# HGRN: the differences of the cumulated log forgets of all eight levels are made by GpSimd in a program of its own

## What is computed

```python
G = jnp.cumsum(gc, axis=2)                       # cumulated log forgets
o_inter = einsum('bhtk,bhkv->bhtv', qc * exp(G), state)
diff = G[:, :, :, None, :] - G[:, :, None, :, :]
decay = exp(where(causal, diff, -inf))
scores = einsum('bhtk,bhsk,bhtsk->bhts', qc, kc, decay)
o_intra = einsum('bhts,bhsv->bhtv', scores, vc)
new_state = exp(G_last) * state + einsum('bhsk,bhsv->bhkv', kc * exp(G_last - G), vc)
```

## Time and profile before

| | before |
|---|---|
| median of three runs | 1599.02 us (1597.28 to 1599.33) |
| span of the profiled execution | 1598.3 us |
| PE busy | 1431.5 us, 90% |
| VectorE busy | 1088.6 us, 68% |
| ScalarE busy | 668.1 us, 42% |
| GpSimd busy | 177.5 us, 11% |
| mean granted clock of TensorE | 0.923 of 2.4 GHz |
| HGRN levels | 1281 to 1353 us of the span |

### The profile page before, as it was taken

The page is one execution under the profiler, slowest core; times in us unless marked ns, Lnnn a source line. Parts: engine busy times, 40 slices in busy tenths (PEclk is TensorE's granted clock), DMA queues, the critical chain, the costliest instruction groups (busy, mean ns, idle before and its releaser), DMA issues.

```text
span 1598.3 us, 19161 instructions
## 1 busy us (share of the span) xinstructions
PE 1431.5 (90%) x6855; PEld 1189.2 (74%) x6855; DVE 1088.6 (68%) x1058; ACT 668.1 (42%) x747; POOL 177.5 (11%) x271
## 2 busy tenths in 40 slices
PE   1876769999799999996899999999998798899998
PEld 1775557888678888774678888788888787778886
DVE  4678774777658886657467775678866698555554
ACT  0433224444254434544353444534446744344442
POOL 1101220111121110210011110211101000100000
PEclk9887778999889999995789999999999899889999
DMA  7741644999468994550168995689954433066671
GB/s 298 259 167 46 229 148 158 310 322 322 155 234 307 342 337 172 185 184 0 53 211 269 315 312 179 223 279 355 336 201 132 146 117 105 27 197 210 211 231 71
DMA packets 183523, 333.96 MB, mean 209 GB/s; under 512 B 8634, under 2 KB 122911, under 8 KB 182322
## 3 DMA queue, kind: packets, MB, share of 16 engines
q1 hardware_dynamic: 157040, 237.95, 44.4%
q0 software_dynamic: 26112, 95.07, 16.6%
q10 hardware_dynamic: 322, 0.27, 0.1%
HBM read 330.64 MB, written 2.62 MB: 209 GB/s over the span
## 4 chain that ended last, share of the span: by engine, by line
PE 73%; DVE 16%; ACT 4%; DMA 3%; issue 2%; POOL 1%; ACTq 0%; DVEq 0%; POOLq 0%
PE ps L1462 67%; DVE wlo L878 2%; DMA ada_raw<-in_w_ada 2%; PE ps L1580 2%; DVE ada_acc L1401 1%; POOL st L415 1%; DVE ada_acc L1027 1%; PE ps L1534 1%; ACT xn L562 1%; DVE xn L943 1%; PE ps L1515 1%; ACT xn L565 1%; DVE ada_acc L897 1%; PE ps L1665 1%; PE ps L1608 1%
## 5 line engine op out<-in xcount | busy, mean ns | idle before, releaser
L878 DVE TENSOR_TENSOR wlo<-raw,whi 128x2048 fp32r<-128x2048 f32 x215 | 490.2, 2285 | 166.0 <-ACT whi L525 166.0
L525 ACT ACTIVATE whi<-raw 128x2048 fp32r<-128x2048 f32 x215 | 409.7, 1909 | 264.1 <-PE ps L1462 241.7
L1462 PE MATMUL ps<-whi,hhi 128*128 128x512 f32 (+1 forms) x1208 | 486.5, 403 | 22.5 <-DVE wlo L878 7.9
L1462 PE MATMUL ps<-wlo,hhi 128*128 128x512 f32 (+1 forms) x1208 | 476.3, 394 | 0.0
L1462 PE MATMUL ps<-whi,hlo 128*128 128x512 f32 (+1 forms) x1208 | 476.2, 394 | 0.0
L1462 PEld LDWEIGHTS ps<-whi,hhi 128*128 128x128 f32 x1208 | 231.2, 191 | 76.5 <-issue 15.7
L1462 PEld LDWEIGHTS ps<-whi,hlo 128*128 128x128 f32 x1208 | 230.7, 191 | 49.3
L1462 PEld LDWEIGHTS ps<-wlo,hhi 128*128 128x128 f32 x1208 | 231.2, 191 | 47.4 <-issue 1.4
L897 DVE SCALAR_TENSOR_TENSOR ada_acc<-ada_raw,csil,ada_acc 128x1024 f32<-128x1024 f32 x120 | 150.4, 1278 | 12.7 <-DMA ada_raw<-in_w_ada 10.3
L1462 PE MATMUL ps<-whi,ahi 128*128 128x512 f32 x400 | 156.1, 390 | 0.0
L1462 PE MATMUL ps<-whi,alo 128*128 128x512 f32 x400 | 155.7, 389 | 0.0
(11 more groups left out here) (233 smaller groups left out, 1387.8 us busy)
## 6 DMA issues: line engine op xcount, KB each, us to landing
raw<-in_ffn_w_in SPq DMA_DIRECT2D x176, 512.0 KB
ada_raw<-in_ada_w POOLq DMA_DIRECT2D x96, 512.0 KB, 5.3
raw<-in_ffn_w_down SPq DMA_DIRECT2D x44, 1024.0 KB
big<-in_ada_w POOLq DMA_DIRECT2D x48, 512.0 KB, 6.7
ada_raw<-in_w_ada POOLq DMA_DIRECT2D x32, 512.0 KB, 4.6
raw<-in_hgrn_w_in SPq DMA_DIRECT2D x16, 1024.0 KB
raw<-in_attn_w_qkv SPq DMA_DIRECT2D x12, 1024.0 KB
raw<-in_w_gate SPq DMA_DIRECT2D x22, 512.0 KB
```

The costliest lines, as they stand in the source:

```text
L525: sc.activation(whi[:, slot, 0:n], raw[:, slot, 0:n], ACT.Copy).then_inc(w_hi, 1)
L878: ve.tensor_tensor(wlo[:, slot, 0:n], raw[:, slot, 0:n], whi[:, slot, 0:n].bitcast(F32), ALU.subtract)\
L1462: done = pe.matmul(dst, lhsT, rhs, start=first and n == 0, stop=final and n == 2, skip_group_check=True)
```

## The change

DVE's function `differences` and its calls are removed. GpSimd gets a function of the same name with the same subtractions, the same places, the same waits (`k_ready`, `lv_mm`) and the same signal (`lv_sub`); it makes all eight levels one after another, behind the set-up of the scan and ahead of the roots of the output norm. Where DVE linked the first two subtractions of level 8, GpSimd does so by a semaphore `lv_first`.

```diff
+            def differences(level):
+
+                E = decayed(level)
+                if level == 1:
+                    pool.wait_ge(k_ready, 2)
+                if level >= 3:
+                    pool.wait_ge(lv_mm, 2 * (level - 1))
+                if level <= len(LEVELS):
+                    n = LEVELS[level - 1]
+                    e, g = halves(E, level), halves(h_G, level)
+                    middle = g[:, :, 0, n - 1:n].to_broadcast((P, HEADS * TOK // (2 * n), n))
+                    done = pool.tensor_tensor(e[:, :, 0, :], middle, g[:, :, 0, :], ALU.subtract)
+                    if level > 1:
+                        done = pool.tensor_tensor(e[:, :, 1, :], g[:, :, 1, :], middle, ALU.subtract)
+                else:
+                    e, g = (a.rearrange("p h (c n) -> p h c n", n=CHUNK) for a in (E, h_G))
+                    total = [g[:, :, c, CHUNK - 1:CHUNK].to_broadcast((P, HEADS, CHUNK)) for c in range(3)]
+                    pool.tensor_tensor(e[:, :, 0, :], total[0], g[:, :, 0, :], ALU.subtract).then_inc(lv_first, 1)
+                    pool.wait_ge(lv_first, 1)
+                    pool.tensor_tensor(e[:, :, 0, :], e[:, :, 0, :], total[1], ALU.add)
+                    pool.tensor_tensor(e[:, :, 1, :], total[1], g[:, :, 1, :], ALU.subtract)
+                    done = pool.tensor_tensor(e[:, :, 3, :], g[:, :, 3, :], total[2], ALU.add)
+                done.then_inc(lv_sub, 1)
+
...
                     pool.memset(flat[:, 0:2 * TOK:CHUNK], 0.0).then_inc(scan_set, 1)
+                    for level in range(1, len(LEVELS) + 2):
+                        differences(level)
                     for t in range(NT):
                         reciprocal_root(sums_v, sums_before(6) + 1 + t, 120 + 8 * t, 8, P, EPS2)
...
                 forget(1)
-                differences(1)
                 lo(U + 9)
                 lo(U + 10)
                 for level in range(len(LEVELS) + 2):
                     if level:
                         decay(level)
                         take_scores(level - 1)
-                        if level <= len(LEVELS):
-                            differences(level + 1)
                     if level <= 7:
                         lo(U + 11 + level)
```

More of the change, by code:

```diff
@@ L271, in two_blocks @@
         q_copied, vg_out, lv_sub, lv_exp, lv_mul = sem("q_copied"), sem("vg_out"), sem("lv_sub"), sem("lv_exp"), sem("lv_mul")
-        lv_mm, lv_copy, g_silu = sem("lv_mm"), sem("lv_copy"), sem("g_silu")
+        lv_mm, lv_copy, g_silu, lv_first = sem("lv_mm"), sem("lv_copy"), sem("g_silu"), sem("lv_first")
         def linked(engine, own):
```

## The result

| kernel | median | runs from to | profiled span | granted clock |
|---|---|---|---|---|
| before (four runs) | 1598.77 us | 1597.28 to 1599.33 | 1598.3 us | 0.923 |
| changed (four runs) | 1608.88 us | 1608.62 to 1610.13 | 1607.0 us | 0.922 |

The changed kernel takes 1.0063 times as long, with a 95% interval of 1.0047 to 1.0079. That is 10.1 us more, beyond the 3.2 us that a measurement of this kernel can tell from no change: slower.

A forecast was written before the change was run, and what follows sets the result against it. PE and DVE were both taken as full in each 9.1 us level. Idle time 8.7 plus clock 4.05 less tail 1.3 gave +11.45 us on 1599.0, so 1610.5 us; forecast's own range 1605 to 1616, overall 1597.3 to 1618.

The forecast's parts named there:

- idle time at levels 2, 4 and 6: PE ahead of scores(2), (4), (6): waits twice the GpSimd price less 1.2, 2.9 us each, 8.7 in all.
- Two full engines: Levels 1 to 7: PE (9.13 us) and DVE (9.12) both full, so removing DVE work alone gains nothing there.
- Exclusive reading: GpSimd reads and DVE's two-SBUF-input instructions exclude each other; DVE waits for the whole GpSimd instruction, in order of asking.
- The price: One 128x1024 subtraction on GpSimd: 2.05 us taken, bounds 1.03 and 3.1 us.
- Who asks first: Level 2: GpSimd asks at 1288.4, DVE's multiplies at 1289.0, so GpSimd goes first; scores(2) at 1296.8 instead of 1293.89.
- the alternation: Levels 2, 4 and 6 each lose 2.9 us; at level 3 GpSimd's reads fall beside masked copies, without delay.
- The end: Level 8: without four half differences on DVE, level 7's masked copy starts at 1347.6 instead of 1348.97; gain 1.3 us.
- The clock: After PE's idle time at levels 2, 4 and 6: lower granted clock costs 1.35 us each, 4.05 in all.
- DVE not waiting: Rival at each level's two multiplies: DVE doesn't wait for GpSimd, only the tail's gain stays, 1597.7 us; chance 0.22.
- Both differences ahead at every level: Rival: GpSimd goes first with both instructions at all levels 2 to 7, +16 us without clock, 1615; chance 0.09.
- GpSimd as the bound: Rival: small groups make GpSimd far slower than 3.1 us a piece, some +30 us over seven levels, 1629; chance 0.09.
- The cheap instruction: Rival: a GpSimd subtraction costs near 1.1 us, leaving +1 to +2 us, 1600.5; chance 0.07.

The follow-up runs named there:

- gp_fill: Changed kernel plus 16 extra 128x128 matmuls nobody needs in PE's idle time ahead of scores(8); 1606.05 us, 1.0047 of the kernel before.
- gp_late: Changed kernel, but GpSimd's differences from level 3 on also wait for DVE's multiplies of the level before; 1599.81 us, 1.0002 of the kernel before.
- gp_copies: Changed kernel with GpSimd's subtractions at levels 1 to 7 replaced by one-input copies; 1601.10 us, 1.0008 of the kernel before.
- gp_writes: Changed kernel with GpSimd's subtractions at levels 1 to 7 replaced by memsets that read nothing; 1596.29 us, 0.9976 of the kernel before.
- gp_late3: Changed kernel, but only the differences of level 3 wait for the multiplies of level 2; 1602.27 us, 1.0020 of the kernel before.
- gp_halves: Changed kernel with each 128x1024 GpSimd subtraction split into two of 128x512; 1601.61 us, 1.0010 of the kernel before.
- dve_tail: Kernel before (differences on DVE) with only the last level's ACT and DVE work reordered; 1598.23 us, 0.9995 of the kernel before.
- gp_late_tail: gp_late with the last level's ACT and DVE work reordered, `lo` of unit 18 last; 1596.34 us, 0.9976 of the kernel before.

## Why the prediction was right

The forecast, 1610.5 us, and its mechanism held. Term by term:

| term | forecast | measured |
|---|---|---|
| idle time at levels 2, 4 and 6 | 3 x 2.9 = 8.7 | 2.31 + 2.85 + 2.39 = 7.55 |
| clock lost in the levels | 3 x 1.35 = 4.05 | 1.62, once (gp_fill's execution: 3.19, twice) |
| tail, scores(7) to scores(8) | -1.3 | -1.30 |
| clock behind scores(8) | none | +2.05 |
| sum | +11.45 | +9.92 |

The measured terms are those of the first trace.

**Two full engines.** That the removal from DVE gives nothing between levels 1 and 7 was nearly right. gp_late has it bare: 9.03 us instead of 9.13 from level 3 on. The step that read PE as the floor at 9.13 was off by 0.1 us a level. The rows fit DVE as the floor: scores(2) started at 1293.89, 0.2 us behind the end of the first of the two masked copies, which began at 1292.44 and took half of 2.49 us, and in the changed kernel, where PE stood idle for that copy, it is the same 0.2 us (1293.30 and 1294.74). Windows that are full on both engines don't say which one is the floor.

**Exclusive reading.** Right, in both directions, which the earlier trace rows showed in one only. In the changed kernel DVE waits for the whole of a GpSimd instruction. The Trainium skill, SBUF — State Buffer, section "Summary: rules for kernel authors", says that the second of the two to issue blocks fully; the changed kernel's trace agrees, 2.92 us for a multiply that takes 1.22 alone. gp_copies and gp_writes show that one read is enough, and that a write isn't.

**The price.** 1.89 to 1.91 us for a first subtraction of 128x1024 against 2.05 taken, within its bounds. With the sum's own rule of twice the price less 1.2, 1.90 gives 2.6 us a level, 7.8 for three; measured 7.55. The three were not alike, 2.31, 2.85 and 2.39 us, because the second subtractions were not: in gp_late, with no two-input instruction of DVE beside them, those of levels 3, 4 and 5 took 2.03, 2.12 and 2.37 us, those of levels 6 and 7 1.89 and 1.90. The one of level 5 falls on the multiplies of level 4, where the idle time was longest. Why its shape costs more is open. The estimate of 2.25 us from the Trainium skill, GPSIMD Engine Reference, section 3.1, would have been further off.

**Who asks first.** The order worked out for level 2, in turns of one instruction each, came as written, and so did the alternation. gp_late3 shows that it is a phase, set once. The turn of level 3 came as written too; at level 5 one multiply was held (2.91 us), which DVE could bear.

**The end.** The term came out as forecast, -1.3 us, in part by luck. Its addends, 1339.6 + 1.9 + 2.2 + 2.3 + 1.2 + 0.2, make 1347.4 and not 1347.6, a gain of nearly 1.6. They allow 7.8 us from scores(7) to scores(8); measured were 8.12, of which 0.25 lie between scores(7) and the start of ACT's high part (1347.23 and 1347.48), and these the forecast had left out.

**The clock.** This is the step that failed in its detail. It priced an idle time from two others of the trace by its length, three times 1.35 us. In two executions one of the three lost clock, 1.62 us, and the two longer ones, 2.80 and 2.33 us, lost none; in a third (gp_fill) the 2.80 us cost 1.63 as well. So length alone doesn't price it. And the forecast didn't look at what a shorter idle time ahead of scores(8) does to the clock behind it: 2.05 us more. Together that is 4.05 us of clock forecast and 3.67 measured (1.62 + 2.05), over half of it at a place that the forecast didn't name. That the total is close is partly luck.

**Rivals.** DVE not waiting falls by 2.92 us for a multiply. Both differences ahead at every level falls by 9.12 us at levels 5 and 7. GpSimd as the bound falls by its 4 to 5.7 us of each level's 9 to 12 us, and the subtractions with the smallest groups, level 7's, cost 1.89 and 1.90 us in gp_late, no more than the cheapest of the rest. The cheap instruction falls by 1.9 us. Each of them would have been seen in the rows that the forecast named.

**Open.** Why 2.14 us at level 2 costs clock in three executions and 2.80 us at level 4 in one of the three, and why 5.61 us ahead of scores(8) leave 15.27 us behind them but 4.0 to 4.4 us 16.9 to 17.6 (gp_copies, gp_halves, dve_tail, gp_late, the changed kernel). The fill runs show that without the idle time the loss is gone, not why its length acts the other way; nor is an idle time enough by itself (3.50 us in gp_writes, and scores(8) at full clock; 3.49 us in gp_late3, and scores(8) in 3.46 us instead of 2.02). The work that PE did before it differs between these kernels, and no run held that fixed. All but the changed kernel's are from one trace each.

## What to carry to other kernels

Before work is moved from DVE to GpSimd, ask what DVE will be running when GpSimd reads: two engines that shut each other out are one engine for those instructions, and the share of idle time on GpSimd says nothing. Place GpSimd's reads by a wait beside DVE's instructions that take their data from PSUM (here one added wait took away the whole loss between the levels), or else make its instructions short, since DVE's wait is one instruction long. Where PE is also full the move buys nothing inside the loop; look at its two ends, and at the clock behind the last idle time before believing a gain there.

## What the runs showed that was not expected

- GpSimd holds DVE as long as its instruction lasts: 1.90 us for most subtractions of 128x1024 (2.37 for one of level 5's), 1.05 us for one of 128x512, about 1.05 for a copy of 128x1024. A memset of 128x1024 (0.95 us) holds nothing. A masked copy whose data comes from PSUM and whose mask from SBUF is hardly held (1.26 us a piece beside GpSimd's subtractions, 1.25 without) and doesn't hold (subtractions of 1.91).
- The wait can hit work that has nothing to do with the move. In the changed kernel a `lo` ahead of the stage took 4.08 us instead of 2.29, behind the second difference of level 2; POOL and DVE:

```profile
1271.61 1.97 POOL L476 TENSOR_TENSOR xn<-big 128x1024 f32<-128x1024 f32 x1
1271.64 4.08 DVE L904 TENSOR_TENSOR wlo<-raw,whi 128x2048 fp32r<-128x2048 f32 x1 [3.61 <-ACT whi L551]
```

- A cause at one level is seen two levels later and again after that, while the level between runs like before. A mean over the stage (72.05 us for seven steps, 10.3 a level) would have hidden both.
- Extra matmuls of no use ahead of the last scores gave back clock behind them: 16 of 128x128 made 13.72 us out of the changed kernel's 17.32; 12, with `lo` moved behind the copy, made 13.76 out of gp_late_tail's 15.25.
- The same program in the same stage lost clock once in two executions and twice in a third. One trace doesn't say where a kernel loses clock.
